# Streaming the columns of six projection blocks in woven orders

## The reference

```
h = RMSNorm(x);  p = h @ w_in            # q, k, v, z, xBC, dt
A = block-sparse causal attention (8 heads x 128)
S = Mamba-2 SSD scan (16 heads x 64), gated with silu(z)
y = concat(RMSNorm(A), GroupRMSNorm(S * silu(z))) @ w_out
x = x + RMSNorm(y)
x = x + RMSNorm(relu(RMSNorm(x) @ w_up)^2 @ w_down)
```

## Time and profile before

| | |
|---|---|
| median of the timed runs | 2174.53 us (2174.19 to 2174.86, 2 runs) |
| span of the profiled execution | 2173.0 us |
| TensorE busy | 2160.4 us (99%), 11445 matmuls |
| DVE busy | 1368.4 us (63%) |
| ACT busy | 1090.3 us (50%) |
| POOL busy | 109.0 us (5%) |
| read from HBM | 401 MB, 186 GB/s over the span |

### The profile page before, as it was taken

One profiled execution on the slowest core, in us unless ns is written; L12 is line 12 of the kernel. 1 busy time (PEld: TensorE's weight loads), 2 busy tenths in 40 slices (PEclk: granted clock), 3 DMA queues, 4 the chain that ended last, 5 costly groups with the idle time before them and its releaser, 6 DMA issues.

```text
span 2173.0 us, 32439 instructions
## 1 busy us (share of the span) xinstructions
PE 2160.4 (99%) x11445; PEld 1856.4 (85%) x11445; DVE 1368.4 (63%) x1633; ACT 1090.3 (50%) x1658; POOL 109.0 (5%) x105
## 2 busy tenths in 40 slices
PE   9999999999999999999999999999999999999998
PEld 8888888888888888888898888888888888888887
DVE  7987564765555465456589975657555645554655
ACT  6554454653454454455465545546434534544543
POOL 2051000000000000000001410000000000000000
PEclk9999999999999999999999999999999999999999
DMA  7655555666665666665556555656666566656564
GB/s 225 180 154 174 155 192 186 198 190 198 191 193 193 192 189 196 192 193 193 179 154 194 156 165 155 197 180 193 205 194 193 181 205 177 208 193 192 177 208 149
DMA packets 232844, 404.34 MB, mean 186 GB/s; under 512 B 12508, under 2 KB 62452, under 8 KB 232244
## 3 DMA queue, kind: packets, MB, share of 16 engines
q1 hardware_dynamic: 231780, 398.57, 59.5%
q10 hardware_dynamic: 720, 4.26, 0.6%
q0 software_dynamic: 256, 0.33, 0.1%
HBM read 401.01 MB, written 2.10 MB: 186 GB/s over the span
## 4 chain that ended last, share of the span: by engine, by line
PE 98%; DMA 1%; issue 1%; DVE 0%; ACT 0%; POOL 0%; POOLq 0%; ACTq 0%; DVEq 0%
PE wide L1009 21%; PE wide L880 16%; PE wide L882 16%; PE wide L881 16%; PE wide L1017 11%; PE wide L956 8%; PE wide L963 4%; PE wide L1146 1%; DMA raw<-in_w_in 0%; PE wide L1048 0%; PE wide L931 0%; PE wide L933 0%; PE wide L934 0%; PE wide L1167 0%; PE wide L1187 0%
## 5 line engine op out<-in xcount | busy, mean ns | idle before, releaser
L1370 DVE TENSOR_TENSOR w_lo<-raw,w_hi 128x1024 fp32r<-128x1024 f32 x752 | 927.1, 1242 | 699.1 <-ACT w_hi L573 657.8
L573 ACT ACTIVATE w_hi<-raw 128x1024 fp32r<-128x1024 f32 x752 | 789.4, 1053 | 509.8 <-PE wide L882 451.3
L880 PE MATMUL wide<-w_hi,u_hi 128*128 128x512 f32 x1280 | 498.5, 389 | 0.0
L882 PE MATMUL wide<-w_hi,u_lo 128*128 128x512 f32 x1280 | 498.0, 389 | 0.0
L881 PE MATMUL wide<-w_lo,u_hi 128*128 128x512 f32 x1280 | 497.9, 389 | 0.0
L1009 PE MATMUL wide<-a_both,w_hi 128*128 128x512 f32 x1778 | 425.2, 389 | 0.0
L1009 PEld LDWEIGHTS wide<-a_both,w_hi 128*128 128x128 f32 x1778 | 333.6, 188 | 64.2
L882 PEld LDWEIGHTS wide<-w_hi,u_lo 128*128 128x128 f32 x1280 | 240.2, 188 | 50.2
L881 PEld LDWEIGHTS wide<-w_lo,u_hi 128*128 128x128 f32 x1280 | 240.3, 188 | 49.7
L880 PEld LDWEIGHTS wide<-w_hi,u_hi 128*128 128x128 f32 x1280 | 240.3, 188 | 49.4
L1017 PEld LDWEIGHTS wide<-a_both,w_lo 128*128 128x128 f32 x2032 | 250.2, 188 | 10.7
(11 more groups left out here) (255 smaller groups left out, 1545.8 us busy)
## 6 DMA issues: line engine op xcount, KB each, us to landing
raw<-in_w_up SPq DMA_DIRECT2D x256, 512.0 KB, 3.9
raw<-in_w_down SPq DMA_DIRECT2D x256, 512.0 KB, 4.5
raw<-in_w_in SPq DMA_DIRECT2D x176, 512.0 KB, 3.7
raw<-in_w_out SPq DMA_DIRECT2D x64, 512.0 KB, 4.4
zg<-in_post_mix_norm ACTq DMA_DIRECT2D x2, 1024.0 KB, 4.8
zg<-in_post_mlp_norm ACTq DMA_DIRECT2D x2, 1024.0 KB, 7.3
out<-x_sb SPq DMA_DIRECT2D x8, 256.0 KB, 2.5
x_sb<-in_x SPq DMA_DIRECT2D x3, 512.0 KB, 8.7
```

Of the source, the lines that this page charges most:

```text
L573: act.activation(w_hi[:, c % RING], raw[:, c % RING], ACT.Copy).then_inc(sem["hi_ready"], 1)
L880: pe.matmul(o, sh, wh, start=(k == 0 and not loaded), stop=False, skip_group_check=loaded)
L882: ins = pe.matmul(o, sl, wh, start=False, stop=(k == KT - 1), skip_group_check=loaded)
L1370: dve.tensor_tensor(lo[:, c % RING], raw[:, c % RING], hi[:, c % RING].bitcast(F32), ALU.subtract).then_inc(sem["split_done"], 1)
```

## The change

A helper `woven` rewrites an operand of 512 neighbouring columns as a pattern of four dimensions: it divides the columns into `parts` equal parts and takes `piece` columns from each part in turn. With (2, 16) the order is columns 0 to 15, 256 to 271, 16 to 31, 272 to 287 and so on. The table `WEAVE` gives the first V block (2, 16), the second (2, 4), the first z block (2, 64), the second (4, 4), the second block of w_out (4, 16) and the third (2, 2). At 4 bytes per column the pieces have 64, 16, 256, 16, 64 and 8 bytes. The moving weights (`w_hi`, `w_lo`) and the output bank are both given the same order, so each column lands where it did. The stationary side, the other blocks and everything else are as before.

```diff
+def woven(a, parts, piece):
+
+    n = a.ap[-1][1] // parts
+    return bass.AP(a.tensor, a.offset, [*a.ap[:-1], [piece, n // piece], [n, parts], [1, piece]])
+
+
+WEAVE = {B_V: (2, 16), B_V + 1: (2, 4), B_Z: (2, 64), B_Z + 1: (4, 4), B_OUT + 1: (4, 16), B_OUT + 2: (2, 2)}
...
-            def token_chunk(c, banks, s_hi, s_lo, tiles=range(TT), loaded=False):
+            def token_chunk(c, banks, s_hi, s_lo, tiles=range(TT), loaded=False, weave=None):
                 for kk, t in itertools.product(range(CK), tiles):
                     k = c * CK + kk
                     wh, wl = (w[:, c % RING, kk * CB:(kk + 1) * CB] for w in (w_hi, w_lo))
                     o = banks[t]
+                    if weave:
+                        wh, wl, o = (woven(a, *weave) for a in (wh, wl, o))
...
                     elif b < B_OUT:
-                        token_chunk(c, acc[b % 2], a_hi, a_lo)
+                        token_chunk(c, acc[b % 2], a_hi, a_lo, weave=WEAVE[b])
                     else:
                         last_half = slot >= MIX_SLOTS - NC // 2
-                        token_chunk(c, acc[b % 2], u_hi, u_lo, (0,) if last_half else range(TT))
+                        token_chunk(c, acc[b % 2], u_hi, u_lo, (0,) if last_half else range(TT),
+                                    weave=WEAVE.get(b))
```

## The result

The changed kernel takes 2211.51 us (2211.27 to 2211.75, 2 runs) against 2174.53 before: a ratio of 1.017, 95% interval 1.014 to 1.020. That is 37 us slower, clear of noise and a little inside the 2% line. It lies in the range I gave and not in the forecast's own: I had taken zero.

What follows compares the result with a forecast made beforehand. TensorE's stream of 512-column matmuls was taken as the bound. Every term of the change was zero, so the profiled span of 2173.0 us plus 1.5 us around it gave 2175 us, range 2169 to 2180, wider range 2170 to 2218.

Steps and rivals of the forecast that it cites:

- the range I gave: Whole kernel: 2170 to 2218 us, holding the central forecast, no effect and slower 8-byte pieces, with 0.84 of the chance.
- the forecast's own: Whole kernel: the central forecast's range, 2169 to 2180 us, 0.25% to either side for the repeat of a run.
- What bounds the kernel: TensorE's stream of 512 columns sets the time: 0.2267 us a matmul, 0.443 ns per column, 98% of the chain.
- The address patterns: Woven matmul instructions: two more operand dimensions cost nothing, showing only if issuing took over 0.22 us.
- the other ports: ACT and DVE writing other ring slots while TensorE reads: the woven stream does not feel them; zero.
- the evictions: ACT and DVE reading the banks after a block's last matmul, in plain order: zero.
- Reading the moving operand: Moving weights of 1152 woven matmuls: bounded between -15.4 us and +234 to +263 us, taken as zero.
- The 8-byte rival: Third output block alone drops towards half rate, larger pieces free: +39 to +44 us, 2214 to 2218; chance 0.11.
- the half-rate row: Plain fp32 matmuls, two passes: 0.43 to 0.455 us for 512 columns, 0.203 to 0.228 us more than now.
- The price per jump: Six woven blocks: each of 112,128 jumps costs a fixed time, +49.7 us at one column's time, +99 at two; chance 0.11.
- The writes: All six woven blocks: any broken-up write to the bank costs, +234 to +263 us, 2408 to 2438; chance 0.03.
- The gain: Woven streams: another order avoids a conflict holding them at 227 rather than 213 ns, up to -15.4 us; chance 0.02.

Runs made afterwards that it cites:

- write_only: Against the changed kernel, only the bank is written in the woven order and the moving operand is read plainly; 2174.79 us, ratio 1.0001.
- all_near: Against the changed kernel, all six woven blocks take one order, (32, 4), 16-byte pieces from 32 parts, read and write; 2171.75 us, ratio 0.9987.
- swapped: Against the changed kernel, the same six orders are given to other blocks among the six, (2, 2) going to the second V block; 2210.88 us.

## Why the prediction was right and wrong

- **What bounds the kernel: right.** TensorE's stream was the bound, the 37.2 us by which it is busy longer are those of the result, and blocks outside the change kept 21.76 to 21.81 us.
- **The address patterns, the other ports and the evictions at nothing: right.** `write_only` has the pattern on the bank and takes 2174.79 us, `all_near` has it on both sides and takes 2171.75; `swapped` shows that what runs beside a block matters by less than 0.5 us.
- **Reading the moving operand, "I take zero": wrong.** This is the step that failed. The row that I took as nearest, 256-column streams at half the price of 512-column ones, says something about one jump, and I let it speak for 32 to 256. It measured 0.05 us for z's 8 pieces, and 0.44 to 10.87 us for the rest. I should also have asked why a column costs 0.443 ns where the granted clock would allow 0.417. I noted that gap and gave it to a rival with a chance of 0.02; the runs show that it is made by the order of reading itself, for in another order it closes to 0.4215 (215.8 / 512).
- **The 8-byte rival: right in its place, wrong in its size and in "alone".** I priced the third output block by the half-rate row at +39 to +44 us. It cost 21.7, since with only two places the stream keeps 338 ns; the half rate comes from four places on. The other 15 us are whole-line orders that this rival had at zero. That 2211.51 lies within 2170 to 2218 is luck: no rival has this make-up, and with the 39 to 44 us that I priced for the third block the other 15 would have carried the time to 2229 to 2233, above the range.
- **The price per jump: wrong.** 147,456 jumps in `all_near` cost less than nothing.
- **The writes: rightly given little.** They cost nothing.
- **The gain: right in its bound.** I had limited it to 13.4 ns a matmul; 10.9 were to be had, but with another order.
- **What the pages said.** The Trainium skill ("SBUF — State Buffer", Specifications) wants two hits per 16-byte line for full bandwidth. Here two hits in a row gave 326 to 490 ns from places 8 or more columns apart, and four in a row 223 to 312: two don't suffice for fp32r columns, unless the next line is the neighbour and both are drawn from in turn (219). The Trainium skill ("TensorE: Matmul & The Clock Gate", Wait — 56ns, not 53.3ns?) gives N / 2.4 GHz + 2.5 ns for matmuls one behind the other, 215.7 ns at 512 columns. The plain order of this kernel misses that by 11 ns; the order in turns meets it with 215.8.

**What stays open.** That the 16-byte line counts is shown by the shifted pieces. That two lines can be drawn from in turn at full pace is shown by the 216 ns. Why whole lines cost 223 to 312 ns depending on the step, why two places are dearer by 13 ns than a plain stream, and why a plain stream doesn't run at 216, I can't tell: neither a price per line, nor one per jump or per return, nor a conflict of address bits fits all of them. Nor is it known why two-column pieces from four places cost 444 ns and single columns from four places 284. Whether bf16 columns behave alike wasn't tried.

## What to carry to other kernels

When streams bind TensorE, compare the measured ns per column with the granted clock. In this kernel a gap of 6% in stretches without waits (0.443 ns against 0.417) was mostly the reading of the moving operand, so try another order there; it is a free choice as long as the reader of the bank undoes it. Reading fp32r columns in turn from two halves gave 4.8% on streams of 512 columns, and undoing it with a step of two in PSUM was free. Keep moving pieces on whole 16-byte lines otherwise, measure the step between them (223 to 312 ns here), and price an order that a trace doesn't hold from a chunk that has it, since neighbouring rows say little.

## What the hardware showed that I had not expected

- A plain contiguous fp32r stream isn't the fastest: 226.7 ns for 512 columns, against 223.4 for 16-byte pieces 64 bytes apart and 215.8 for single columns in turn.
- Writing PSUM in the six orders, down to pieces of 8 bytes, and reading it with a step of two from DVE, cost nothing (2174.79 us, and 683 ns).
- A start shifted by one column costs a contiguous stream 6 to 9 ns (236 against 227 to 230).
- The rate never fell much below half: 512 single columns in turn from 8 or more places took 431 to 490 ns, no more than pieces of two.
